# Two expert weight loads cut into sixteen DMAs of eight rows each

## The reference, cut to what matters

```
for e in range(8):
    out = out + combine[:, e] * ((silu(t @ w_gate[e]) * (t @ w_up[e])) @ w_down[e])
```

## Time and profile before

| | |
|---|---|
| time, median of 3 runs | 1258.43 us (1257.62 to 1258.66) |
| the profiled execution's own time | 1257.88 us |
| its span, first to last instruction | 1256.0 us |
| busy, of the span | PE 96%, weight loads (PEld) 58%, VectorE (DVE) 31%, ScalarE (ACT) 19%, GpSimd (POOL) 6% |
| DMA packets, bytes | 80,343, 429.21 MB |
| granted TensorE clock, mean | 0.993 |

### The profile page before, as it was taken

How to read it: one execution, slowest core, us unless ns; L and a number is a source line. 1 busy time by engine, 2 the same in 40 slices (tenths; PEclk the granted TensorE clock), 3 DMA queues, 4 the chain that set the end, 5 groups by cost and what they waited for, 6 DMA issues and landing times.

```text
span 1256.0 us, 28582 instructions
## 1 busy us (share of the span) xinstructions
PE 1202.0 (96%) x13164; PEld 725.6 (58%) x13164; DVE 388.8 (31%) x725; ACT 240.3 (19%) x353; POOL 78.0 (6%) x78
## 2 busy tenths in 40 slices
PE   9999999999999999988998999999999999999675
PEld 7888888888876436434335644643553464455233
DVE  6977766577765111011002012000201200020121
ACT  6674443353652100000010010001001000100001
POOL 3000000000100000100100100010010001001000
PEclk9999999999999999989999999999999999999999
DMA  9646663666239999999999999999999999999994
GB/s 317 238 135 201 201 193 113 217 189 215 89 120 357 429 423 400 404 424 427 408 424 425 419 417 422 425 409 424 425 416 418 425 424 409 425 424 413 422 423 179
DMA packets 80343, 429.21 MB, mean 342 GB/s; under 512 B 5222, under 2 KB 41808, under 8 KB 55648
## 3 DMA queue, kind: packets, MB, share of 16 engines
q1 hardware_dynamic: 74736, 417.70, 82.7%
q0 software_dynamic: 5072, 8.59, 2.6%
q10 hardware_dynamic: 416, 1.09, 0.2%
HBM read 421.06 MB, written 6.31 MB: 340 GB/s over the span
## 4 chain that ended last, share of the span: by engine, by line
PE 78%; DMA 16%; issue 2%; DVE 2%; ACT 1%; POOL 0%; POOLq 0%; SPq 0%; DVEq 0%
PE bank L1843 77%; DMA late_area<-in_moe_w_up 5%; DMA late_area<-in_moe_w_down 5%; DMA late_area<-in_moe_w_gate 4%; DMA sum_dram<-qT,slot_row 1%; PE bank L1886 0%; PE bank L2083 0%; ACT work L1086 0%; ACT h L1086 0%; POOL split_area L921 0%; DVE split_area L708 0%; DVE h L1817 0%; DVE work L1581 0%; POOL sum_dram L944 0%; DVE split_area L1334 0%
## 5 line engine op out<-in xcount | busy, mean ns | idle before, releaser
L1843 PE MATMUL bank<-late_area 128*32 128x448 f32 (+1 forms) x5280 | 408.4, 467 | 30.4 <-DMA late_area<-in_moe_w_up 18.6
L1843 PE MATMUL bank<-raw_area,late_area 128*32 128x448 f32 (+1 forms) x5280 | 404.0, 464 | 8.0 <-DMA raw_area<-in_moe_w_up 6.1
L1843 PEld LDWEIGHTS bank<-late_area 128*32 128x32 f32 x5280 | 192.9, 110 | 241.8 <-issue 176.0
L1843 PE MATMUL bank<-split_area 128*128 128x512 f32 (+1 forms) x1848 | 331.0, 339 | 1.1 <-DVE split_area L1334 0.8
L1843 PEld LDWEIGHTS bank<-raw_area,late_area 128*32 128x32 f32 x5280 | 194.0, 109 | 208.5 <-issue 155.4
L1843 PEld LDWEIGHTS bank<-split_area 128*128 128x128 f32 x1848 | 283.4, 189 | 42.6 <-issue 4.1
L708 DVE TENSOR_TENSOR split_area<-raw_area,split_area 128x2048 fp32r<-128x2048 f32 (+1 forms) x56 | 122.6, 2193 | 47.0 <-ACT split_area L686 47.0
L1705 DVE COPY slot_sum<-next_sum 128x9 f32<-128x9 f32 x8 | 1.4, 173 | 405.7 <-DMA sum_dram<-qT,slot_row 389.7
L686 ACT CAST split_area<-raw_area 128x2048 fp32r<-128x2048 f32 (+1 forms) x59 | 107.7, 1833 | 72.3 <-PE bank L1843 70.0
L1216 ACT COPY qT<-bank 128x512 f32<-128x512 f32 x8 | 4.7, 587 | 562.4 <-PE bank L1843 562.4
L1729 DVE SCALAR_TENSOR_TENSOR work<-bank,slot_sum,work 128x448 f32<-128x448 f32 x44 | 30.1, 684 | 225.0 <-PE bank L1843 220.3
(11 more groups left out here) (217 smaller groups left out, 419.0 us busy)
## 6 DMA issues: line engine op xcount, KB each, us to landing
raw_area<-in_moe_w_gate SPq DMA_DIRECT2D x32, 1792.0 KB, 23.7
late_area<-in_moe_w_gate SPq DMA_DIRECT2D x32, 1792.0 KB, 24.3
raw_area<-in_moe_w_up SPq DMA_DIRECT2D x32, 1792.0 KB, 25.4
late_area<-in_moe_w_up SPq DMA_DIRECT2D x32, 1792.0 KB, 25.6
raw_area<-in_moe_w_down SPq DMA_DIRECT2D x32, 1792.0 KB, 25.3
late_area<-in_moe_w_down SPq DMA_DIRECT2D x32, 1792.0 KB, 24.5
raw_area<-in_sb_w_qkv SPq DMA_DIRECT2D x12, 1024.0 KB, 5.2
raw_area<-in_ffn_w_down SPq DMA_DIRECT2D x11, 1024.0 KB, 4.8
```

Of the source, the lines that this page charges most:

```text
L1843: return nc.tensor.matmul(out, lhsT, rhs, start=start, stop=stop, **kw)
```

## The change

The first gate load (m = 0) of items 4 and 6 is issued as 16 DMAs, each of eight rows into eight partitions, in place of one DMA of 128 rows into 128 partitions. The bytes, their source and their place in the buffer are the same, and so is the wait before them. Each of the 16 adds 16 to the buffer's semaphore, so that such a load adds 256 where it added 16; the new function `landed` gives PE the counts with the 240 more for each such load that has gone before or is being waited for.

```diff
+EIGHT = 8
+BY_EIGHTS = ((0, 4), (0, 6))
+
+def landed(m, i):
+    pieces = sum(n == m % SLOTS and (not isinstance(i, int) or item <= i) for n, item in BY_EIGHTS)
+    return i * LANDED[-1] + (LANDED[m // SLOTS] + pieces * 16 * (P // EIGHT - 1))
...
                     slot, arrived = slots[m % SLOTS], load_full[m % SLOTS]
+                    if isinstance(i, int) and (m, i) in BY_EIGHTS:
+                        for p0 in range(0, P, EIGHT):
+                            r0 = m * P + p0
+                            src = a["moe_w_gate"][0][bass.ds(e, 1), r0:r0 + EIGHT, :].rearrange("o d f -> (o d) f")
+                            sp.dma_start(slot[p0:p0 + EIGHT, :], src).then_inc(arrived, 16)
+                        continue
...
-                pe.wait_ge(load_full[m % SLOTS], i * LANDED[-1] + LANDED[m // SLOTS])
+                pe.wait_ge(load_full[m % SLOTS], landed(m, i))
```

## The result

The changed kernel takes 1294.63 us (median of four runs, 1292.57 to 1297.13) beside 1258.05 us (1257.62 to 1258.66) for the kernel before in the same comparison: ratio 1.0287, 95% interval 1.0275 to 1.0299. It is 36.6 us slower. The forecast was 1268.8, so the sign was right and the size was less than a third; 1294.6 lies outside the range too. The profiled execution has a span of 1293.7 us.

The account below looks back on a forecast made before the run. The last DMA row's landing was taken to bound the kernel. Leaders carrying two cut loads lose 2 x 10.9 = 21.8 us, ending 10.4 after 1241.2: 1268.3 on the profiled execution, median 1268.8; range 1255.0 to 1279, the forecast's own 1262 to 1279.

Parts of the forecast that it names:

- What bounds the kernel: At the end: the last DMA row's landing, at 1241.16 us, sets the time; a microsecond there is one of the total.
- 4.33 us more for them: In each cut load: eight engines carry 16 rows each, others none; 4.33 us more for carriers, 4.33 less for the rest.
- Issue, 7 to 8.3 us, hidden: On SP: 16 issues per cut load take 7 to 8.3 us, covered by some 20 us of queued loads; cost 0.
- What a row costs: Eight engines writing eight partitions: from nothing extra (0.54 us a row) to 69 us for 16 pieces.
- Sharing: In cut loads: engines writing the same partitions slow each other; carriers lose 10.9 us per load, others gain nothing; chance 0.42.
- near its low end: Sharing's size in cut loads: half a carrier's rows at half speed, 4.3 us more, plus 2.2 from the other eight.
- Leaders or laggers: Which engines carry pieces: the eight that finish at 1229.8 us (leaders) or the eight 11.4 us later (laggers).
- The sum: At the end: leaders as carriers lose 21.8 us, ending at 1251.6, 10.4 after 1241.2; forecast 1268.8 us.
- 6.6 us of slack: At PE in item 4: load 0 lands at 813.4, its use began at 820.0, so the slack holds.
- The free ride: Rival: pieces ride on leaders, writes don't hold each other up; last row 2.7 us earlier, 1255.7 us; chance 0.29.
- nothing moves: Rival: pieces spread over all 16 engines, each still carrying 8 rows of the load; 1258.4 us; chance 0.17.
- Laggers with sharing: Rival: laggers carry the pieces and sharing holds; last row 21.8 us later, 1280.2 us; chance 0.11.

Follow-up runs that it names:

- Every fourth partition: Changed kernel, both cut loads still 16 DMAs of eight rows, each taking every fourth row into every fourth partition of a group of 32: 1282.83 us, ratio 1.0183.
- the kernel with partitions 0 to 63 alone: Of the changed kernel's two cut loads only rows and partitions 0 to 63 loaded, in eight DMAs, partitions four apart: 1257.46 us, ratio 0.9996.
- the run in 16 neighbours: Changed kernel with both cut loads whole in 8 DMAs of 16 neighbouring rows and partitions in place of 16 of eight: 1284.35 us, ratio 1.0202.
- load 0 of item 0: Cuts moved from items 4 and 6 to item 0: load 0 every fourth partition, load 1 eight neighbours; 1268.49 us beside 1259.75, one run each.

## Why the prediction was wrong, point by point

- *What bounds the kernel.* Right. The end is the landing of the last load, before and after, and the profiled span grew by what that landing grew, 37.7 us.
- *A row is one packet on one engine; eight engines carry; 4.33 us more for them, 4.33 less for the others.* Right: eight counts per piece, and the kernel with partitions 0 to 63 alone moved nothing but the others' 8.7 us.
- *Issue, 7 to 8.3 us, hidden.* Right: 7.61 and 7.22 us, and PE is busy for all of 803 to 810 behind it. Every fourth partition makes the issues dearer (13.81 us for 16), still hidden.
- *What a row costs.* This is the step that failed. Sharing was taken as a matter between the engines that meet: a carrier loses 10.9 us per load, "and the others, whose saved rows still go into their partitions beside their own, gain nothing". In fact such meetings hold all 16 engines to their pace. The two late carriers' last rows end 35.9 us later (37.7 with what lies behind them), 18 per load, of which 4.3 are their own rows and 13.6 the common slowness; the run in 16 neighbours, where no engine has extra rows, gives 12.9 per load for it. An engine that carries nothing is slowed too and has only its 4.3 to set against it. The bounds were wide enough (nothing extra to 69 us for 16 pieces), and "near its low end" was the wrong choice in them.
- *Leaders or laggers.* The sum and the rivals took the carriers as all leaders or all laggers. They are six and two. The two decide the end; had all eight been leaders, the end would lie at about 1262 to 1266, where the fourteen others finish, 21 to 25 us after 1241.2. By this estimate, of the 27.3 us that the forecast's 10.4 fell short of 37.7, the size of the sharing is 10 to 14 and the mixed carriers the other 13 to 17. Mixed carriers stood in none of the rivals. Two late carriers would have made the kernel 8.7 us slower even with free writes, so that the sign came out right is in part luck.
- *The signs.* The share, which was to fall "under 0.95 in items 4 and 6", was the wrong sign: it stayed at 1.0, and the rate fell. Loads 1 to 7 of item 4 were to take about 5 us longer from issue to landing; they took 40.2 and 41.5 us (medians of loads 1 to 3 and 4 to 7) where they had taken 24.6 and 25.2, about 16 more. PE waits in item 6 came, and in item 4 also, where 6.6 us of slack was thought to hold. The idle stretch at the end, put at half the engines for 10 us (20 for laggers), came as 14 engines for some 13 us.
- *The rivals.* The free ride and "nothing moves" are refuted by the half rate. The free ride would have failed with leaders alone as well: two engines on one group at 1.08 us a row move 26.5 GB/s, no more than one does, so a row carried by a leader into a lagger's partitions takes the lagger's own time. Laggers with sharing, 1280.2, was nearest, by a mechanism half right.
- *The two rules weighed.* The Trainium skill's page "DMA: Bandwidth & Descriptors" (Why a DMA increments its semaphore by 16 and not by 1) gave eight engines and the same eight each time, and the runs agree. Its page "SBUF — State Buffer" (Door 1: The DMA port swizzle) gave, as an estimate, 2.1 us a piece alone and 34 us for 16 in lockstep; measured were 1.72 us alone and 2.29 beside plain loads, and 32 us for the 16 (357 to 389). The sum stood on a milder figure than that estimate.
- *Slips in the working.* The 13th slice moves 357 GB/s, and 400 or more begins with the 14th; 4.3 + 4.3 + 2.2 is 10.8, not 10.9. Neither changes the forecast by more than 0.2 us.

Left open: why engines that write partitions of their own are held up by a meeting elsewhere. The runs show that it happens when two engines meet two others, begins and ends with the meeting, and does not depend on the source rows; which part of the path is shared was not tried. That the laggers lag because of instruction fetches was not tried either. No run points to a version that beats the kernel before: moving rows from late engines to early ones means writing partitions that the late ones fill.

## What to carry to other kernels

Read the rate beside the share: a DMA share of 1.0 at half the usual GB/s is a place where engines stand in each other's way, and a drop by half with all 16 busy cannot come from a few of them alone. Here whole loads of 128 partitions ran at 424 GB/s together; DMAs of eight or 16 neighbouring rows sent engines into the partitions of others, and slowed every transfer in flight until the last of them was out. If loads must be cut, keep each engine in the partitions that it fills in a whole load (here eight rows four apart in partitions 0 to 63 were free), or cut where the other engines are idle and stay so until the pieces are through (load 0 of item 0 ran at nearly full pace, load 1 met plain loads and lost 9.7 us).

## What the runs showed of the hardware that had not been expected

- Two engines in the partitions of two others slow all 16 DMA engines: 207 GB/s in place of 410 to 430, with twelve engines uninvolved.
- Two engines on one group of partitions share 26 GB/s (1.08 to 1.1 us a row); four engines on four neighbours reach 33 GB/s (1.72 us a row) when nothing else runs, and all 16 engines together 100 GB/s when plain loads run beside them.
- Eight rows 16 partitions apart (1296.6 us) cost as much as eight neighbours (1294.6); four apart cost a third less (1282.8).
